# Rotary lane swap as a stream shuffle, and the last down projection's weight sums as adding DMAs

## What is computed

```python
# first block
h = rms_norm(x, pre_mix_norm[l])
proj = h @ w_in[l]
q, k, v_a, u, v_s = jnp.split(proj, [512, 1024, 1536, 2048], axis=-1)
q = partial_rotary(q.reshape(B, S, ATTN_HEADS, HEAD_DIM), positions).transpose(0, 2, 1, 3)
k = partial_rotary(k.reshape(B, S, ATTN_HEADS, HEAD_DIM), positions).transpose(0, 2, 1, 3)
attn = dilated_mixture_attention(q, k, v_a)
# end of the second block
h = rmsnorm(x, norm_ffn[i])
x = x + jnp.square(jax.nn.relu(h @ w_up[i])) @ w_down[i]
return rmsnorm(x, norm_final)
```

## Time and profile before

| | |
|---|---|
| median of 3 runs | 1827.9 us (1827.61 to 1828.93) |
| the profiled execution | 1827.18 us, its span 1825.3 us |
| PE busy | 1791.4 us (98%) |
| PEld busy | 1453.7 us (80%) |
| DVE busy | 1139.5 us (62%) |
| ACT busy | 834.0 us (46%) |
| POOL busy | 279.2 us (15%) |
| DMA | 205.69 MB, mean 113 GB/s |

### The profile page before, as it was taken

One profiled execution on the slowest core, in us unless ns is written; L12 is line 12 of the kernel. 1 busy time (PEld: TensorE's weight loads), 2 busy tenths in 40 slices (PEclk: granted clock), 3 DMA queues, 4 the chain that ended last, 5 costly groups with the idle time before them and its releaser, 6 DMA issues.

```text
span 1825.3 us, 24686 instructions
## 1 busy us (share of the span) xinstructions
PE 1791.4 (98%) x9602; PEld 1453.7 (80%) x9602; DVE 1139.5 (62%) x1779; ACT 834.0 (46%) x1593; POOL 279.2 (15%) x356
## 2 busy tenths in 40 slices
PE   7999999999999999999999999999999999999998
PEld 7767898888888877878878786667788998888886
DVE  6356544233345787887768745677556358686958
ACT  5255533222234565554555544554434445342435
POOL 0502100000000045254462640000020000000000
PEclk9999999999999999999999999999999999999999
DMA  7211332322331443352443444233544241404121
GB/s 244 81 59 38 106 127 94 114 93 92 93 92 59 167 140 129 117 149 100 155 139 116 142 159 150 82 105 115 139 150 134 70 155 59 157 28 162 61 90 47
DMA packets 128388, 205.69 MB, mean 113 GB/s; under 512 B 26496, under 2 KB 58688, under 8 KB 127632
## 3 DMA queue, kind: packets, MB, share of 16 engines
q1 hardware_dynamic: 118944, 166.70, 28.7%
q0 software_dynamic: 8464, 34.93, 5.3%
q10 hardware_dynamic: 864, 2.49, 0.3%
HBM read 191.37 MB, written 12.71 MB: 112 GB/s over the span
## 4 chain that ended last, share of the span: by engine, by line
PE 79%; DVE 13%; ACT 3%; issue 3%; POOL 1%; DMA 0%; DVEq 0%; ACTq 0%; POOLq 0%
PE m L2139 14%; PE m L2141 14%; PE m L2140 14%; PE m L2150 6%; PE m L2152 6%; PE m L2151 6%; PE s L2302 3%; DVE lo L1395 3%; PE m L2274 2%; PE m L2276 1%; PE m L2275 1%; PE s L2298 1%; PE m L2247 1%; PE m L2249 1%; PE m L2248 1%
## 5 line engine op out<-in xcount | busy, mean ns | idle before, releaser
L2139 PE MATMUL m<-hH,hi 128*128 128x512 f32 (+1 forms) x1392 | 531.5, 382 | 2.9 <-DVE hL L1425 1.6
L2141 PE MATMUL m<-hH,lo 128*128 128x512 f32 (+1 forms) x1392 | 509.8, 366 | 0.0
L2140 PE MATMUL m<-hL,hi 128*128 128x512 f32 (+1 forms) x1392 | 508.9, 366 | 0.0
L1395 DVE TENSOR_TENSOR lo<-raw,hi 128x1024 fp32r<-128x1024 f32 x267 | 333.8, 1261 | 170.0 <-ACT hi L915 169.8
L915 ACT ACTIVATE hi<-raw 128x1024 fp32r<-128x1024 f32 x267 | 276.1, 1050 | 181.3 <-PE m L2141 44.3
L2139 PEld LDWEIGHTS m<-hH,hi 128*128 128x128 f32 x1392 | 263.3, 189 | 49.8 <-issue 5.4
L2141 PEld LDWEIGHTS m<-hH,lo 128*128 128x128 f32 x1392 | 263.1, 189 | 43.4
L2140 PEld LDWEIGHTS m<-hL,hi 128*128 128x128 f32 x1392 | 263.7, 189 | 39.9 <-issue 1.0
L2150 PE MATMUL m<-hi,hH 128*128 128x512 f32 (+1 forms) x320 | 134.8, 421 | 1.6 <-DVE lo L1395 1.6
L2152 PE MATMUL m<-hi,hL 128*128 128x512 f32 (+1 forms) x320 | 122.1, 381 | 0.0
L2151 PE MATMUL m<-lo,hH 128*128 128x512 f32 (+1 forms) x320 | 121.9, 381 | 0.0
(11 more groups left out here) (330 smaller groups left out, 2894.3 us busy)
## 6 DMA issues: line engine op xcount, KB each, us to landing
raw<-in_w_in_dram SPq DMA_DIRECT2D x72, 512.0 KB, 3.7
hn<-scr_cs_dram POOLq DMA_DIRECT2D x32, 512.0 KB, 4.1
raw<-in_w_up_dram SPq DMA_DIRECT2D x32, 512.0 KB, 5.0
wq<-in_w_down_dram SPq DMA_DIRECT2D x24, 512.0 KB, 8.2
raw<-in_w_gate_dram SPq DMA_DIRECT2D x44, 256.0 KB, 2.8
raw<-in_w_up_dram SPq DMA_DIRECT2D x44, 256.0 KB, 3.1
raw<-in_w_down_dram SPq DMA_DIRECT2D x22, 512.0 KB, 4.0
raw<-in_w_in_dram SPq DMA_DIRECT2D x33, 256.0 KB, 3.0
```

The lines of the kernel that those rows point to most:

```text
L1395: e.tensor_tensor(d, r, h.bitcast(F32), ALU.subtract).then_inc(s_lo, 1)
L2139: e.matmul(bank, wh[:, kk, c], h[:, k, q], start=k == 0, stop=False)
L2140: e.matmul(bank, wh[:, kk, c], l[:, k, q], start=False, stop=False)
L2141: x = e.matmul(bank, wl[:, kk, c], h[:, k, q], start=False, stop=k == kt - 1)
```

## The change

The rotation's swap is done by VectorE: a stream shuffle, which permutes the lanes within each group of 32 partitions, copies the tile with its lanes swapped into `ta`, and the product with RS is then made in place there. The wait of GpSimd's product for the swap stays, on the same semaphore. TensorE's part and the permutation in the constants go.

The weight sums are done by DMAs from GpSimd's queue that add to their destination. The four buffer pairs are called `a`, `b`, `c`, `d` and run through states: `d` is loaded with b22, then b11, b12 and b21 are added in turn; `a` is b11, then + b12; `b` is b12, then + b22; `c` is b21, then b22. All sums are arranged as additions, and two of the seven products (`FS_MINUS`) are then subtracted from X instead of added, and the hidden sums change signs to match. A state other than the first comes from another 512 KB read of `w_down_2` for each half: 12 DMAs a block, of which 10 add and 2 overwrite. SP loads the first states, in the order `d`, `b`, `a`, `c`.

```diff
+SWAP = [(m + 8) % 16 for m in range(16)] + list(range(16, 32))
...
-FS_W = ["b11", "b21", "b11", "b11", "b12", "b22", "b21"]
-WQ_I = {"b11": 0, "b21": 2, "b22": 4, "b12": 6}
-
-FS_T = [("t3", 0, -11), ("t3", 1, -9), ("t2", 0, -7), ("t2", 1, -5), ("t4", 0, -3), ("t4", 1, -2), ("t1", 0, 5), ("t1", 1, 7)]
+FS_MINUS = (2, 4)
+
+FS_W = ["a", "c", "d", "a", "b", "c", "d"]
+WQ_I = {"a": 0, "b": 2, "c": 4, "d": 6}
+WQ_PER = {"a": 2, "b": 2, "c": 2, "d": 4}
+FS_READY = [("a", 1), ("c", 1), ("d", 3), ("a", 2), ("b", 2), ("c", 2), ("d", 4)]
+FS_LATER = [("d", 2, (1, 1), None), ("d", 3, (1, 2), None), ("b", 2, (2, 2), None), ("a", 2, (1, 2), 0), ("c", 2, (2, 2), 1), ("d", 4, (2, 1), 2)]
+FS_D_AT = when([s0(f"fs{f}") + s for f in range(NFF2) for s in (-30, -24, -22, -2, -1, 2)])
...
                     r = WQ[WQ_I[w] + x]
-                    if u // 2 in (0, 1, 5):
-                        o.wait_ge(s_wq[WQ_I[w] // 2], WQ_FROM + 32 * f[0] + 32)
-                    else:
-                        o.wait_ge(s_ts, 8 * f[0] + FS_TN[{2: "t2", 3: "t1", 4: "t3", 6: "t4"}[u // 2], x])
+                    o.wait_ge(*landed(f[0], *FS_READY[u // 2]))
...
-                    e.tensor_tensor(x, bank[:, :], x, ALU.add).then_inc(s_evd, 1)
+                    if i // 2 in FS_MINUS:
+                        e.tensor_tensor(x, x, bank[:, :], ALU.subtract).then_inc(s_evd, 1)
+                    else:
+                        e.tensor_tensor(x, bank[:, :], x, ALU.add).then_inc(s_evd, 1)
...
-                    e.tensor_tensor(FS2, fa(2, 2), fa(2, 1), ALU.subtract).then_inc(s_as, 1)
+                    e.scalar_tensor_tensor(out=FS2, in0=fa(2, 1), scalar=-1.0, in1=fa(2, 2), op0=ALU.mult, op1=ALU.subtract).then_inc(s_as, 1)
...
                 for i in ROPE_AT.get(g - 1, ()):
+                    b = BLK["q" if i < 4 else "k"]
+                    o.wait_ge(s_eva, EVACUATED[b.e0 + i % 4][1])
+                    if i >= 2:
+                        o.wait_ge(s_rope, i - 1)
+                    e.stream_shuffle(TA[2 + i % 2][:, :], (Q if i < 4 else K)[:, i % 4, :], SWAP).then_inc(s_sw, 1)
                     o.wait_ge(s_sw, i + 1)
                     o.wait_ge(s_rsf, 1)
-                    if i >= 2:
-                        o.wait_ge(s_rope, i - 1)
-                    e.tensor_tensor(TA[2 + i % 2][:, :], side[i % 2][:, :], RS[:, :], ALU.mult).then_inc(s_swp, 1)
+                    e.tensor_tensor(TA[2 + i % 2][:, :], TA[2 + i % 2][:, :], RS[:, :], ALU.mult).then_inc(s_swp, 1)
...
+            def later_quarters(g):
+
+                for i in FS_D_AT.get(g, ()):
+                    f, (w, n, (j, c), p) = i // 6, FS_LATER[i % 6]
+                    u0 = BLK[f"fs{f}"].u0
+                    o.wait_ge(*landed(f, w, n - 1))
+                    for x in range(2):
+                        if p is not None:
+                            o.wait_ge(s_lo, u0 + 2 * p + x + 1)
+                        src = rows(A["w_down_2"][0], 4 * f + 2 * (j - 1) + x, 512 * c - 512, 512 * c)
+                        if w == "c":
+                            e.dma_start(WQ[WQ_I[w] + x], src).then_inc(s_wd[WQ_I[w] // 2], 16)
+                        else:
+                            e.dma_start(WQ[WQ_I[w] + x], src, accum_op=ALU.add).then_inc(s_wd[WQ_I[w] // 2], 16)
...
-                    claim("side", i % 2)
-                    o.wait_ge(s_cst, 16)
-                    o.wait_ge(s_eva, EVACUATED[b.e0 + i % 4][1])
-                    e.matmul(side[i % 2][:, :], CST[:, C_PERM:C_PERM + 128], (Q if i < 4 else K)[:, i % 4, :], start=True, stop=True).then_inc(s_sw, 1)
-                    read["side", i % 2] = (s_swp, i + 1)
```

More of the change, by code:

```diff
@@ L52, in constants @@
     c[:, C_ID:C_ID + 128] = np.eye(128)
[L53 to L58, removed]
     for n, delta in enumerate((3, 2, 1, 0)):
@@ L425 @@
 FS_FRESH = (0, 1, 3)
-FS_W = ["b11", "b21", "b11", "b11", "b12", "b22", "b21"]
-WQ_I = {"b11": 0, "b21": 2, "b22": 4, "b12": 6}
-FS_T = [("t3", 0, -11), ("t3", 1, -9), ("t2", 0, -7), ("t2", 1, -5), ("t4", 0, -3), ("t4", 1, -2), ("t1", 0, 5), ("t1", 1, 7)]
-FS_TN = {(t, x): i + 1 for i, (t, x, _) in enumerate(FS_T)}
-FS_T_AT = when([s0(f"fs{f}") + s for f in range(NFF2) for _, _, s in FS_T])
+FS_MINUS = (2, 4)
[5 more added lines that the diff above has]
+FS_D_AT = when([s0(f"fs{f}") + s for f in range(NFF2) for s in (-30, -24, -22, -2, -1, 2)])
 FS_S_AT = when([s0(f"fs{f}") + s for f in range(NFF2) for s in (-14, 1, 2, 3)])
@@ L547, in build @@
         s_osq, s_og, s_orc = sem("s_osq"), sem("s_og"), sem("s_orc")
-        s_ts, s_as = sem("s_ts"), sem("s_as")
+        s_as = sem("s_as")
+        s_wd, WD_FROM = s_os, 64
         s_wq, WQ_FROM = s_x, 16
@@ L677, in fa, with landed @@
             return FA[j - 1][:, :, 256 * i - 256:256 * i]
+        def landed(f, w, n):
+            if n == 1:
+                return s_wq[WQ_I[w] // 2], WQ_FROM + 32 * f + 32
+            return s_wd[WQ_I[w] // 2], WD_FROM + 32 * ((WQ_PER[w] - 1) * f + n - 1)
         def rows(w, u, c0, c1):
@@ L796, in load_quarter @@
             def load_quarter(f, i):
-                w, u0 = ("b11", "b21", "b22", "b12")[i], BLK["fs0"].u0 if f == 0 else BLK[f"fs{f - 1}"].u0
-                j, n = int(w[1]) - 1, int(w[2]) - 1
+                w, j, n = (("d", 1, 1), ("b", 0, 1), ("a", 0, 0), ("c", 1, 0))[i]
+                u0 = BLK["fs0"].u0 if f == 0 else BLK[f"fs{f - 1}"].u0
                 for x in range(2):
@@ L804, in load_quarter @@
                     else:
-                        o.wait_ge(s_lo, u0 + {"b11": 6, "b21": 12, "b22": 10, "b12": 8}[w] + x + 1)
+                        o.wait_ge(s_lo, u0 + {"a": 6, "b": 8, "c": 10, "d": 12}[w] + x + 1)
                     e.dma_start(WQ[WQ_I[w] + x], rows(A["w_down_2"][0], 4 * f + 2 * j + x, 512 * n, 512 * n + 512)).then_inc(s_wq[WQ_I[w] // 2], 16)
@@ L1554, in sum_hidden @@
                     o.wait_ge(s_flo, HID + 8 * f + 3)
[L1555 to L1580, removed]
+                    e.tensor_tensor(fa(1, 2), fa(1, 2), FS2, ALU.add).then_inc(s_as, 1)
             added = {}
@@ L1928, in vector_program @@
                     sum_hidden(i)
-                for i in FS_T_AT.get(g, ()):
-                    sum_weights(i)
                 for m in P_AT.get(g - 1, ()):
@@ L2103, in gpsimd_program @@
                         e.dma_start(MEMX[:, t, :], A["mem_2"][0, 128 * t:128 * t + 128, :]).then_inc(s_mem[t], 16)
+                later_quarters(g)
                 for k in MG_AT.get(g, ()):
@@ L2315, in mixture @@
             def mixture(g):
-                for i in ROPE_AT.get(g, ()):
-                    b = BLK["q" if i < 4 else "k"]
-                    claim("side", i % 2)
-                    o.wait_ge(s_cst, 16)
-                    o.wait_ge(s_eva, EVACUATED[b.e0 + i % 4][1])
-                    e.matmul(side[i % 2][:, :], CST[:, C_PERM:C_PERM + 128], (Q if i < 4 else K)[:, i % 4, :], start=True, stop=True).then_inc(s_sw, 1)
-                    read["side", i % 2] = (s_swp, i + 1)
                 for b in WT_AT.get(g, ()):
```

## The result

The changed kernel takes **1817.4 us** (median of 4 runs, 1815.64 to 1819.24) against 1827.76 us (1825.92 to 1828.93, 4 runs) for the kernel before in the same session: ratio 0.9949, 95% interval 0.9936 to 0.9961. The forecast was 1818.1, in a range of 1815.5 to 1823.5. The execution profiled here took 1819.24 us around a span of 1817.4 us, so it is at the slow end of its own runs, and its span is 7.9 us under the span before of 1825.3.

A forecast was written before the change was run, and what follows sets the result against it. TensorE, busy 98% of 1825.3 us, was taken as the bound. From the 1827.9 us median, -7.0 (swap) + 1.1 (K chain) - 3.9 (weight sums) = -9.8 gave 1818.1 us, with an 8-in-10 range of 1815.5 to 1823.5.

The forecast's parts named there:

- The swap on TensorE: Q and K rotation: eight float32 permutation products leave TensorE, 0.87 us of its path each, 7.0 us gained.
- The K chain: K rotation to second scores: VectorE and GpSimd exclude each other, stall 1.4 us against 0.29, 1.1 us given back.
- Rival A: K rotation: the chain isn't slowed by the shared port; 11.2 us gained, 1816.7 us; chance 0.14.
- The weight sums: Last down projection: 32 sums leave VectorE, three TensorE gaps close in each of four blocks, 3.9 us gained.
- rival B: Last down projection: gaps pass to ScalarE or an adding DMA's landing; 1820 to 1822.0 us; chance 0.21.
- Hence nothing: Last down projection: the added DMAs land early enough for their readers, so they cost no time.
- GpSimd's 0.59 us an issue: GpSimd's queue: issuing the added DMAs costs 0.59 us each, 7 us a block, on an otherwise idle engine.
- The landing: Adding DMAs of the last down projection: taken to land in 8 to 12 us, bounded by 3.5 and 24.
- the prediction's sign of being wrong: Last down projection: adding pairs landing over 15 us with ScalarE waiting on them would show the forecast wrong.
- The slack of the fourth state: Last adding pair of d: 15.3 us free before ScalarE takes it, late for TensorE only after 24 us.
- rival C: Adding DMAs are slow, deciding from 24 us a pair; gain used up at 26.5 us a pair; chance 0.08.
- Rival D: Rotation: an equal TensorE wait replaces the swap, only 3.9 us gained, 1824.0 us; chance 0.10 with mixtures up to 1826.

The follow-up runs named there:

- e1: The kernel before with only the rotation's swap moved to VectorE, weight sums left on VectorE: 1821.74 us, ratio 0.9973.
- e5: The changed kernel with the shuffled tile written to a PSUM bank, so the product with RS reads one PSUM operand: 1815.75 us, ratio 0.9936.
- e9: The changed kernel, unaltered, measured once more in the second session: 1816.75 us, ratio 0.9943.
- e2: The changed kernel with the permutation product put back on TensorE, so only the weight sums by adding DMAs remain: 1822.87 us, ratio 0.9976.
- e6: The changed kernel with the 40 adding DMAs made plain loads of the same bytes: 1816.42 us, ratio 0.9942.
- e8: The changed kernel with the last adding pair (fourth state of d) waiting for the fifth product's units, not the third's: 1828.98 us, ratio 1.0012.

## Why the prediction was right

**The swap on TensorE, -7.0 us: right, measured -7.2** (0.90 us each, not 0.87). The eight swaps are gone, the starts are 0.23 us apart where they stood, and e1 gives 5.7 us for the whole part, against 5.9 by the sum. Pricing a removed instruction by starts (0.87 us) and not by its 2 x 592 ns was the step that mattered: by durations it would have been 9.5 us.

**The K chain, +1.1 us: right, measured +1.27.** The layout put GpSimd's last sum at 81.3 in the clock of before, 77.8 in that of after; it ended at 77.77. The stretched products and sums (1.61 to 2.29 us) are those that the two rows of before foretold. Rival A, no exclusion, is refuted in after and shown in e5, where it is made true by an operand in PSUM. The shuffle took 0.72 to 0.75 us against 0.69.

**The weight sums, -3.9 us: right, measured -4.3** in the `fs` blocks. All three gaps of each block closed (4 x 0.99 is 4.0, not 3.9), and no other engine took their place there, so rival B fell. What I hadn't in the sum was -0.9 us at the end, +1.7 us (1.05 in e9, none in e5) for the new gaps, and +1.1 us for the clock fall, if it belongs to the change. They cancel in part, and that the forecast lies within 0.7 us of the measured time is to that extent luck. With e2's 4.6 us the part is 0.7 better than the 3.9 forecast. That the new gaps exist was missed at the sentence "Hence nothing": the adding DMAs were weighed only against their own readers, not against the `w_up` loads that share the DMA engines with them, and on which ScalarE, in order, hangs its evacuations. The issue of the `w_up` loads moved little and mostly forward: beside TensorE's own progress the first two called in `fs1` go out 1.7 us earlier than before, the third 0.7 us earlier and the fourth 0.2 us later. Their landings moved, from 6.5 to 10.0 us in the stretch shown.

**GpSimd's 0.59 us an issue: undersized.** An adding DMA took 1.2 to 3.7 us to issue (median 1.5), a plain one of 512 KB 0.72 us in e6. It was free all the same. The landing, taken as 8 to 12 us, was 10.2 in the median; some took over 15 us, the prediction's sign of being wrong, but ScalarE's rounding in the `fs` blocks never waited for a DMA.

**The slack of the fourth state: wrong, with no effect on the forecast.** "Late for TensorE only after 24 us" followed only the unit from ScalarE to TensorE. e8 shows that the cost comes earlier and by other users of the same conversion: SP's next load into the buffers, and what is queued behind it on SP, ScalarE and VectorE. The first step of it held: ScalarE wants unit 12 15.4 us after `lo` of unit 5 ends (1627.41 - 1612.0 in after; 15.3 predicted). In e8 the unit is there 21.5 us after that (1635.65 - 1614.14), so under the 24 us from which rival C charged anything, and it costs 12.2 us. So rival C decides earlier than it said. Where between 15.4 and 21.5 us the cost begins was not measured.

**Rival D**, an equal wait in place of the swap, fell: after Q's slots no wait appears, and for K it is 1.27 us and not 3.5.

## What to carry to other kernels

Price what leaves the bounding engine by its starts, and add for the chain that was hidden behind it: lay that chain out with the stretched durations that the trace already shows where two engines meet. For a load that is to come later, follow every reader and every later writer of its buffer, and what is queued behind each of them on every engine in order; the slack of the first reader says little. Two SBUF operands on VectorE beside GpSimd can be avoided by letting the step before write to PSUM (e5), and the two versions with it have the lowest medians, 1815.3 and 1815.8 us. The times don't set them apart from the changed kernel's: the intervals overlap, and both profiled executions also had the shorter first 20 us.

## What the runs showed of the hardware

A stream shuffle of 128x512 in float32 can write PSUM and takes 0.68 to 0.69 us there, 0.72 to 0.75 us into SBUF; loading its mask shows as 0.01 us. An adding DMA of 512 KB makes 272 packets and a plain one 144 (e6); it lands at 10.2 against 7.3 us in this kernel. And a stall of TensorE of 2.1 or 2.2 us costs nearly double when it is followed by 4 us at a granted clock of 0.65 and 0.57, as in two of three blocks of e8; in the third, with a stall of the same length (2.1 us), the clock stayed at 1.00. In the state-space stage the same pause of 5 us, busy for 2.2, is followed by a fall in after and by none in before. What decides between the two these runs don't show.
